# HGRN scores on TensorE: decay levels that share one loaded weight in pairs

## The reference, cut to what matters

```python
b = jnp.cumsum(lf_i, axis=1)
diff = b[:, :, None] - b[:, None, :]                 # decay from frame s to frame t
diff = jnp.where(tri[None, :, :, None, None], diff, -jnp.inf)
att = jnp.einsum('bthd,btshd->bhts', q_i, jnp.exp(diff) * k_i[:, None])
intra = jnp.einsum('bhts,bshe->bthe', att, v_i)
```

## Time and profile before

| | |
|---|---|
| Median of 3 runs | 2650.66 us (2640.95 to 2654.57) |
| Span of the profiled execution | 2647.1 us |
| PE busy | 2570.6 us (97%) |
| DVE / ACT / POOL busy | 1246.3 / 673.9 / 458.7 us |
| Mean granted TensorE clock | 0.988 |
| Idle time of PE before line 738 with DVE's ATT as releaser | 22.4 us in 11 places |

### The profile page before, as it was taken

How to read it: one execution, slowest core, us unless ns; L and a number is a source line. 1 busy time by engine, 2 the same in 40 slices (tenths; PEclk the granted TensorE clock), 3 DMA queues, 4 the chain that set the end, 5 groups by cost and what they waited for, 6 DMA issues and landing times.

```text
span 2647.1 us, 38662 instructions
## 1 busy us (share of the span) xinstructions
PE 2570.6 (97%) x14936; PEld 2453.3 (93%) x14936; DVE 1246.3 (47%) x2290; ACT 673.9 (25%) x1257; POOL 458.7 (17%) x680
## 2 busy tenths in 40 slices
PE   7999999999999999999999999999999999999998
PEld 6999999999999989999999999987998998998997
DVE  4043424325366566666576534455433333333335
ACT  5123222322212212222222233233221221221221
POOL 1011102002153353363364300001100000000000
PEclk9999999999999999999999999999999999999999
DMA  4251615234243223223133353322210110110114
GB/s 152 92 178 60 221 60 188 96 116 158 68 141 121 85 89 108 95 92 118 65 112 122 108 197 118 125 88 80 64 48 24 55 48 24 55 48 24 55 40 151
DMA packets 219034, 257.27 MB, mean 97 GB/s; under 512 B 8208, under 2 KB 186640, under 8 KB 218768
## 3 DMA queue, kind: packets, MB, share of 16 engines
q1 hardware_dynamic: 218896, 255.31, 28.9%
HBM read 175.06 MB, written 80.22 MB: 96 GB/s over the span
## 4 chain that ended last, share of the span: by engine, by line
PE 80%; DVE 11%; issue 6%; ACT 1%; DMA 1%; POOL 1%; SPq 0%; DVEq 0%; POOLq 0%; ACTq 0%
PE bank L585 11%; PE bank L587 11%; PE bank L586 11%; PE bank L832 5%; PE bank L833 5%; PE bank L834 5%; PE bank L903 5%; PE bank L901 5%; PE bank L902 5%; DVE QE L1375 3%; DVE PP L1376 3%; PE bank L746 3%; PE bank L862 1%; PE bank L861 1%; PE bank L860 1%
## 5 line engine op out<-in xcount | busy, mean ns | idle before, releaser
L585 PE MATMUL bank<-XH,WHI 128*128 128x384 f32 x2304 | 797.3, 346 | 22.3 <-issue 13.3
L587 PE MATMUL bank<-XH,WLO 128*128 128x384 f32 x2304 | 778.6, 338 | 0.0
L586 PE MATMUL bank<-XL,WHI 128*128 128x384 f32 x2304 | 778.1, 338 | 0.0
L585 PEld LDWEIGHTS bank<-XH,WHI 128*128 128x128 f32 x2304 | 439.7, 191 | 29.0 <-issue 14.0
L586 PEld LDWEIGHTS bank<-XL,WHI 128*128 128x128 f32 x2304 | 439.9, 191 | 1.1
L587 PEld LDWEIGHTS bank<-XH,WLO 128*128 128x128 f32 x2304 | 438.2, 190 | 0.0
L917 ACT ACTIVATE ZST<-bank 128x384 f32<-128x384 f32 x240 | 117.9, 492 | 843.3 <-PE bank L587 842.6
L1211 DVE TENSOR_TENSOR WLO<-WRAW,WHI 128x1024 fp32r<-128x1024 f32 x128 | 170.3, 1331 | 223.6 <-ACT WHI L917 218.4
L832 PE MATMUL bank<-XH,WHI 128*128 128x384 f32 x768 | 257.5, 335 | 3.6 <-ACT XH L917 3.6
L834 PE MATMUL bank<-XH,WLO 128*128 128x384 f32 x768 | 257.3, 335 | 0.0
L833 PE MATMUL bank<-XL,WHI 128*128 128x384 f32 x768 | 257.3, 335 | 0.0
(11 more groups left out here) (180 smaller groups left out, 3421.6 us busy)
## 6 DMA issues: line engine op xcount, KB each, us to landing
scratch_z<-ZST SPq DMA_DIRECT2D x80, 576.0 KB, 2.8
WRAW<-in_w_in SPq DMA_DIRECT2D x80, 512.0 KB, 4.2
HZ<-scratch_z SPq DMA_DIRECT2D x32, 576.0 KB, 4.9
WRAW<-in_w_up SPq DMA_DIRECT2D x32, 512.0 KB, 4.0
WRAW<-in_w_down SPq DMA_DIRECT2D x32, 512.0 KB, 3.2
MG<-scratch_z SPq DMA_DIRECT2D x16, 576.0 KB, 5.7
ZQ<-scratch_z SPq DMA_DIRECT2D x4, 1152.0 KB, 6.7
ZK<-scratch_z SPq DMA_DIRECT2D x4, 1152.0 KB, 8.6
```

Source lines behind the costliest of these rows:

```text
L585: pe.matmul(psum[c][:, 0:CH], WHI[p][:, k, :], XH[:, k, s], start=(k == 0), stop=False)
L586: pe.matmul(psum[c][:, 0:CH], WHI[p][:, k, :], XL[:, k, s], start=False, stop=False)
L587: last = pe.matmul(psum[c][:, 0:CH], WLO[p][:, k, :], XH[:, k, s], start=False, stop=(k == KT - 1))
```

## The change

PE: `KE` keeps four weights instead of seven: for levels 0 and 1 together, 2 and 3 together, 4 and 5 together, and 6. The lower level of a pair uses the weight as it is. At the upper level the sources in the first quarter of the block miss the decay over the second quarter; so Q has two versions there, one for each half of the sources, and the second is the first times that decay (kept in `FS`). The diagonal's matmul takes only the even frames (64 columns with step 2), since the weight of levels 0 and 1 at an odd frame is K itself. Moving widths in a tile are 64, 128, 192, 192 and 64 columns (in the last tile 64, 128 and 192). The pair of levels 4 and 5 goes to bank PT right behind the transposes, and `H.t_full` is raised after it, before the other score matmuls.

DVE: `prep_q` copies Q for level 0 instead of multiplying it, adds a small copy to FS at levels 2 and 4 (24 and up to 6 elements), makes it wait for the product before PP is updated, and adds a product `qa` at levels 3 and 5. `weights` takes nine sources of scores instead of eight (eight COPY_PREDICATED after the base instead of seven; in the last tile still four), with a new table MB in place of the identity, and doesn't wait for `H.kv` in the last tile.

POOL: `prep_k` makes the weights of levels 1, 2 and 4 over all 384 (or 256) columns and waits for each, that of level 6 over half as before, and none at levels 0, 3 and 5. SP loads one more table at the start, and the first group's inputs of the next stage in two DMAs more.

```diff
@@ constants @@
+KES = 4
+QES = 9
@@ tiles @@
-        KE = [sb(f"KE{i}", [P, LEV, CH], F32, ph) for i in range(2)]
+        KE = [sb(f"KE{i}", [P, KES, CH], F32, ph) for i in range(2)]
+        UAX = [sb(f"UAX{i}", [P, 3, CH], F32, ph) for i in range(2)]
-        QE = [sb(f"QE{i}", [P, LEV, CH // 2], F32, ph) for i in range(2)]
+        QE = [sb(f"QE{i}", [P, QES, CH // 2], F32, ph) for i in range(2)]
+        FS = sb("FS", [P, 32], F32, ph)
@@ hg_a @@
-                tr = pe.transpose(PT[:, P:2 * P], KRH[:, s], ident[:, :])
-                if t == NT - 1:
-                    tr.then_inc(H.t_full, 1)
-                last = pe.matmul(PSC[:, 0:P], KK[:, s], HZ[0][:, s], start=True, stop=True, skip_group_check=True)
                 kt = slice(r * P, (r + 1) * P)
                 qt = slice(r * 64, (r + 1) * 64)
-                for l in range(min(6, LEV if t < NT - 1 else LEVS)):
-                    last = pe.matmul(PSC[:, P + 64 * l:P + 64 * (l + 1)], KE[c % 2][:, l, kt], QE[c % 2][:, l, qt],
-                                     start=True, stop=True, skip_group_check=True)
+                last = pe.transpose(PT[:, P:2 * P], KRH[:, s], ident[:, :])
+                if t < NT - 1:
+                    last = pe.matmul(PT[:, 2 * P:2 * P + 192].rearrange("p (l n) -> p l n", l=3), KE[c % 2][:, 2, kt],
+                                     QE[c % 2][:, 5:8, qt], start=True, stop=True, skip_group_check=True)
+                last.then_inc(H.t_full, 1)
+                pe.matmul(PSC[:, 0:64], KK[:, s], HZ[0][:, t * P:(t + 1) * P:2], start=True, stop=True,
+                          skip_group_check=True)
+                last = pe.matmul(PSC[:, 64:192].rearrange("p (l n) -> p l n", l=2), KE[c % 2][:, 0, kt],
+                                 QE[c % 2][:, 0:2, qt], start=True, stop=True, skip_group_check=True)
+                last = pe.matmul(PSC[:, 192:384].rearrange("p (l n) -> p l n", l=3), KE[c % 2][:, 1, kt],
+                                 QE[c % 2][:, 2:5, qt], start=True, stop=True, skip_group_check=True)
+                if t < NT - 1:
+                    last = pe.matmul(PSC[:, 384:448], KE[c % 2][:, 3, kt], QE[c % 2][:, 8, qt], start=True, stop=True,
+                                     skip_group_check=True)
                 last.then_inc(H.sc, 1)
-                if t < NT - 1:
-                    last = pe.matmul(PT[:, 2 * P:2 * P + 64], KE[c % 2][:, 6, kt], QE[c % 2][:, 6, qt], start=True, stop=True)
-                    last.then_inc(H.t_full, 1)
@@ prep_q @@
-                    q = QE[c % 2][:, l, 0:n // 2].rearrange("p (g w) -> p g w", w=w)
+                    j = (0, 1, 2, 3, 5, 6, 8)[l]
+                    qa = QE[c % 2][:, j + 1, 0:n // 2].rearrange("p (g w) -> p g w", w=w) if l in (3, 5) else None
+                    q = QE[c % 2][:, j, 0:n // 2].rearrange("p (g w) -> p g w", w=w)
                     pp = v(PP)
-                    dve.tensor_tensor(q, v(HZ[0])[:, :, 1, :], pp[:, :, 1, :], ALU.mult)
+                    if l in (2, 4):
+                        dve.tensor_copy(FS[:, 12 * l - 24:12 * l - 24 + n // (4 * w)], PP[:, c * CH + 2 * w - 1:c * CH + n:4 * w])
+                    if l in (2, 4):
+                        ch(dve.tensor_tensor(q, v(HZ[0])[:, :, 1, :], pp[:, :, 1, :], ALU.mult))
+                    elif l:
+                        dve.tensor_tensor(q, v(HZ[0])[:, :, 1, :], pp[:, :, 1, :], ALU.mult)
+                    else:
+                        dve.tensor_copy(q, v(HZ[0])[:, :, 1, :])
                     ch(dve.tensor_tensor(pp[:, :, 1, :], pp[:, :, 1, :],
                                          pp[:, :, 0, w - 1:w].to_broadcast([P, n // (2 * w), w]), ALU.mult))
+                    if l in (3, 5):
+                        fs = FS[:, 12 * l - 36:12 * l - 36 + n // (2 * w)]
+                        dve.tensor_tensor(qa, q, fs.unsqueeze(2).to_broadcast([P, n // (2 * w), w]), ALU.mult)
@@ weights @@
-                dve.wait_ge(H.kv, 9 * h + t + 2)
+                if t < NT - 1:
+                    dve.wait_ge(H.kv, 9 * h + t + 2)
-                ch(dve.tensor_tensor(at[:, :], PSC[:, 0:P], ident[:, :], ALU.mult))
-                for l in range(LEV if t < NT - 1 else LEVS):
-                    w = 1 << l
-                    src = PSC[:, P + 64 * l:P + 64 * (l + 1)] if l < 6 else PT[:, 2 * P:2 * P + 64]
+                ch(dve.tensor_tensor(at[:, :].rearrange("p (g a) -> p a g", a=2),
+                                     PSC[:, 0:P].rearrange("p (a g) -> p a g", a=2), MB[:, :, :], ALU.mult))
+                for j in (1, 2, 3, 4, 8, 5, 6, 7) if t < NT - 1 else (1, 2, 3, 4):
+                    w = 1 << (0, 1, 2, 3, 3, 4, 5, 5, 6)[j]
+                    x = 64 + 64 * j
+                    src = PSC[:, x:x + 64] if j < 5 else PSC[:, 384:448] if j == 8 else PT[:, x - 128:x - 64]
...
@@ prep_k @@
-                    pool.tensor_tensor(v(KE[c % 2][:, l, :])[:, :, 0, :], v(KK[:, s])[:, :, 0, :], rr[:, :, 0, :], ALU.mult)
+                    if l in (1, 2, 4):
+                        ch(pool.tensor_tensor(KE[c % 2][:, l // 2, 0:n], KK[:, c * CH:c * CH + n], RR[:, c * CH:c * CH + n],
+                                              ALU.mult))
+                    elif l == 6:
+                        pool.tensor_tensor(v(KE[c % 2][:, 3, :])[:, :, 0, :], v(KK[:, s])[:, :, 0, :], rr[:, :, 0, :],
+                                           ALU.mult)
```

More of the change, by code:

```diff
@@ L119, in program @@
         ones = sb("ones", [P, P], F32, pa)
-        MK = sb("MK", [P, LEV, 64], U32, pa)
+        MK = sb("MK", [P, QES - 1, 64], U32, pa)
+        MB = sb("MB", [P, 2, 64], F32, pa)
         RM = sb("RM", [P, NS], F32, pa)
@@ L162, in program @@
         UA = [[HZ[k // NC][:, k % NC * CH:(k % NC + 1) * CH] for k in range(KT - 1)] + [URAW[:, :]]] + \
-            [[KE[i][:, k, :] for k in range(LEV)] + [HZ[2][:, (i + 1) * CH:(i + 2) * CH]] for i in range(2)]
+            [[KE[i][:, k, :] for k in range(KES)] + [UAX[i][:, k, :] for k in range(3)] +
+             [HZ[2][:, (i + 1) * CH:(i + 2) * CH]] for i in range(2)]
         ph.close()
@@ L384, in _ @@
             sp.dma_start(MK[:, :, :], a["c_mask"]).then_inc(c_in2, 16)
+            sp.dma_start(MB[:, :, :], a["c_base"]).then_inc(c_in2, 16)
             sp.dma_start(RM[:, :], a["c_rows"]).then_inc(c_in2, 16)
@@ L456, in load_ua @@
                     cs = slice(c * CH, (c + 1) * CH)
-                    sp.dma_start(KE[c - 1][:, :, :], us[0:LEV, :, cs].rearrange("k p t -> p k t")).then_inc(ua_in[c], 16)
-                    sp.dma_start(UA[c][LEV], us[LEV, :, cs]).then_inc(ua_in[c], 16)
+                    sp.dma_start(KE[c - 1][:, :, :], us[0:KES, :, cs].rearrange("k p t -> p k t")).then_inc(ua_in[c], 16)
+                    sp.dma_start(UAX[c - 1][:, :, :], us[KES:KT - 1, :, cs].rearrange("k p t -> p k t")).then_inc(ua_in[c], 16)
+                    sp.dma_start(UA[c][KT - 1], us[KT - 1, :, cs]).then_inc(ua_in[c], 16)
             ret_mixed(sp)
@@ L1053, in kz_hg @@
                     act.activation(KM8[b], PT[:, P:2 * P], ACT.Copy, scale=RM[:, b:b + 1]).then_inc(H.kz8, 1)
-            act.wait_ge(c_in2, 48)
+            act.wait_ge(c_in2, 64)
             def forget(h):
@@ L1065, in piece @@
                 if i < 3 * KT:
-                    act.wait_ge(ua_in[c], 32 if c else 64)
+                    act.wait_ge(ua_in[c], 48 if c else 64)
                     copy(XH[:, k, cs], UA[c][k]).then_inc(sp_hi, 1)
@@ L1315, in rotate_k0 @@
                 ch(dve.tensor_tensor(KR[:, 0, s], RTMP[:, 0, :], RTMP[:, 1, :], ALU.subtract))
-            dve.wait_ge(c_in2, 48)
+            dve.wait_ge(c_in2, 64)
             with dve.Fori(0, RH) as h:
@@ L1385, in weights @@
                 dve.wait_ge(H.st_full, 10 * h + (t if t >= 2 else 1))
-                dve.wait_ge(H.kv, 9 * h + t + 2)
+                if t < NT - 1:
+                    dve.wait_ge(H.kv, 9 * h + t + 2)
                 at = ATT[t % 2]
-                ch(dve.tensor_tensor(at[:, :], PSC[:, 0:P], ident[:, :], ALU.mult))
-                for l in range(LEV if t < NT - 1 else LEVS):
-                    w = 1 << l
-                    src = PSC[:, P + 64 * l:P + 64 * (l + 1)] if l < 6 else PT[:, 2 * P:2 * P + 64]
+                ch(dve.tensor_tensor(at[:, :].rearrange("p (g a) -> p a g", a=2),
[4 more added lines that the diff above has]
+                    src = PSC[:, x:x + 64] if j < 5 else PSC[:, 384:448] if j == 8 else PT[:, x - 128:x - 64]
                     g = lambda x: x.rearrange("p (g w) -> p g w", w=w)
                     last = dve.copy_predicated(at[:, :].rearrange("p (g a w) -> p g a w", a=2, w=w)[:, :, 1, :],
-                                               g(MK[:, l, :]), g(src))
-                    if l < (LEV if t < NT - 1 else LEVS) - 1:
+                                               g(MK[:, j - 1, :]), g(src))
+                    if j != (7 if t < NT - 1 else 4):
                         ch(last)
@@ L1615, in gate @@
```

(16 more changed lines are left out.)

## The result

The changed kernel takes 2673.65 us (median of 4 runs, 2673.16 to 2675.95), the kernel before 2649.06 us (median of 4 runs, 2640.95 to 2654.57): ratio 1.0098, 95% interval 1.0077 to 1.0118. The profiled execution has a span of 2671.4 us, 24.3 us longer. PE is busy for less (2548.1 us against 2570.6), as it was meant to be, and waits for more.

A forecast was written before the change was run, and what follows sets the result against it. PE was taken to bound most of a head, DVE slot 13 to tile 1. +26 us over eight heads and +10 for the clock made +36, so 2686 us; own range 2664 to 2710, overall 2638 to 2714.

The forecast's parts named there:

- What bounds the kernel: HGRN stage: PE bounds most of a head, but from slot 13 to tile 1 DVE sets the pace.
- PE's part: Score matmuls on PE: 0.43 us saved a tile, 0.32 in a head's last, 30 us in all.
- Rival 4: Score matmuls on PE: the wide ones gain nothing, +17 us, 2703 us; chance 0.05.
- DVE's part, c = 0 and 1: prep_q on DVE, first two groups: added products, tiny copies and waits cost 1.8 us a call.
- I count that as even: prep_k on POOL: 1.0 us less a call, but each of three wider products holds DVE longer; no net effect.
- Slot 13 to tile 1: DVE's stretch of a head: two prep_q calls 3.6 us plus one predicated copy 0.28, +3.9 us.
- Tile 4 to 5: Stretch of a head where DVE's longer prep_q part and merge decide: 8.9 us against 7.46, +1.45 us.
- sum by head: Changes of a head's five stretches added: +3.2 us a head, times 8 heads +26 us.
- The clock: Half clock behind PE's longer waits before tile 1 and at the stage's start: +10 us, bounds +2 and +25.
- The sum: Whole kernel: +26 us from the heads and +10 from the clock, +36 us on the span.
- the forecast's own range: Whole kernel: 2664 to 2710 us, from 1.0 to 2.6 us a prep_q call and clock +5 to +18.
- Rival 1: Prep stretches: DVE and POOL act as one queue, a call grows 0.3 us instead of 1.8; 2643 us, chance 0.17.

The follow-up runs named there:

- experiment 1: Changed kernel without the copies to FS, the products qa and the two waits that it adds to prep_q on DVE: 2636.0 us, ratio 0.9952.
- experiment 3: Changed kernel with POOL's prep_k(h, 1) held back until DVE has finished prep_q(h, 1): 2619.04 us, ratio 0.9890.
- 5: Kernel before, with the second part of prep_q(h, 1) moved from slot 1 to slot 4, behind the merge of tile 1: 2612.52 us, ratio 0.9862.
- experiment 2: Kernel before with only the DVE instructions added to prep_q, products into a scratch tile: 2688.93 us, ratio 1.0151.
- experiment 6: Changed kernel with the second part of prep_q(h, 1) moved from slot 1 to slot 4, behind the merge of tile 1: 2613.44 us, ratio 0.9863.
- (8): Changed kernel with POOL's prep_k(h, 1) held back and prep_q(h, 2) and slot 6's weight split rearranged behind merges in slots 5 to 7: 2595.81 us, ratio 0.9797.
- (9): Kernel before with POOL's prep_k(h, 1) held back and prep_q(h, 2) and slot 6's weight split rearranged behind merges in slots 5 to 7: 2612.38 us, ratio 0.9873.

## Why the prediction was right, point by point

- **What bounds the kernel.** Right. DVE's chain from slot 13 to tile 1 sets the head. This stretch makes 2.6 of the 4.5 us a head that experiment 1 takes off, 5.1 of 6.9 in experiment 3, 3.0 of 4.8 in 5, and 2.4 of the 5.4 that experiment 2 adds; most of the rest is the half clock behind it and tiles 4 and 5.
- **PE's part.** Predicted 0.43 us a tile and 0.32 in the last, measured 0.44 (tile 2 to 3 was 880.16 - 873.32 = 6.84 us, and is 6.40) and 0.34: 31 us for 30. Rival 4 (wide matmuls gain nothing) is out.
- **DVE's part, c = 0 and 1.** Predicted 3.6 us in both calls, measured in head 1 1.2 (12.3 to 13.5) and 2.6 (9.6 to 12.2), 3.8, and 3.5 in the mean of heads 1 to 7. The sum was right, its parts less so, and that they cancel is in part luck. The products `qa` took what was put on them (L1401, 0.607 us). The tiny copies took 0.56 us in the mean of these calls instead of 0.25, since a copy also stands behind POOL. The copy in place of level 0's product, put at -0.1, took 0.73 us where the product had 0.65. Against that, some old products got shorter (L1392, which now stands behind a copy, 0.355 us in the mean where L1375 had 0.610). I read this as DVE's sequence meeting POOL's in another order, so that only the sum of a call can be carried over; no run varies the order alone.

```profile
L1390 DVE COPY FS<-PP 128x24 f32<-128x24 f32 x24 | 16.6, 693 | 0.8
L1401 DVE TENSOR_TENSOR QE<-QE,FS 128x192 f32<-128x192 f32 x40 | 24.3, 607 | 1.4
L1392 DVE TENSOR_TENSOR QE<-HZ,PP 128x192 f32<-128x192 f32 x40 | 14.2, 355 | 0.0
```

- **"I count that as even"** (POOL's fewer but wider products). Nearly right: by experiment 1 the calls are as long with wide products as with narrow ones (21.5 and 21.6 us); by experiment 2 the wide ones cost at most 0.8 us a head more.
- **Slot 13 to tile 1**, +3.9 predicted, +3.4 measured. The two calls grew by 3.5 of the 3.6 us, and the merge by 0.2 and not 0.28 us: eight COPY_PREDICATED take 2.15 us where seven took 1.95. What the rest went to isn't shown; the kernel before has heads of 29.6 to 34.0 us here, and the changed one 34.1 to 35.4. This is the smaller of two mis-sized terms.
- **Tile 4 to 5**, +1.45 predicted, +0.8 measured. The mis-sized step is part 1 of c = 2: it grew from 4.5 to 5.4 us (894.37 to 899.81), by 1.0 and not 1.25 us. The merge grew less, as above, and two of the seven heads had a wait of 0.4 us here already, which the sum by head 1 didn't count.
- **The clock**, +10 predicted. What half clock cost can be read against the same stretches without it (tile 1 to 2: 6.65 us before, and 6.18 in experiment 6, since the changed kernel has none without it; tile 5 to 8: 20.44 after). Over heads 0 to 7 it cost 12.2 us before, all of it behind tile 1, and 16.6 behind tile 1 and 6.4 behind tile 5 after: +10.8. So the size was right, but not the place: the prediction put all of it behind tile 1 and at the stage's start. The rise came less behind tile 1 (+4.4), where in the longer waits part of the half clock falls on a PE that stands, than behind the new waits before tile 5 in four heads (+6.4). A reading was wrong too: four of the eight waits before tile 1 had no half clock behind them (1.65, 2.64, 0.61 and 2.09 us), not three, since one of the five stretches stands at the stage's start (757.6 to 764.4 us).
- **The sum.** +36 predicted, +24.6 measured (2673.65 - 2649.06), inside the forecast's own range; PE's wait for the merged scores came to 64 us, not to about 75. Since the clock's term came out, nearly all that is missing stands in the sum by head: 3.2 us predicted, 2.9 measured with the clock in it, and 1.7 without (8.6 of the clock's 10.8 us fall on heads 1 to 7). Rival 1, even or slightly faster by the shared access, had the access right but not its effect: DVE's two calls grew by 3.5 us, although POOL had less to do: POOL ended its `prep_k` for c = 1 0.9 to 6.1 us behind DVE's call before the change, and ends it 0.4 to 2.0 us ahead of it now. The rival's working was also off: 4 x 0.2 less 1.0 is -0.2, not the 0.3 us a call that it went on with.

## What to carry to other kernels

Before a change that trades matmuls for vector instructions, look for the place at which PE waits with the same releaser in every head. What the other engine gets in addition there is paid at once (here 3.4 us a head for 3.7 us of added work), whatever the busy shares (PE 97%, DVE 47%) say. Then look at whether two engines prepare for the same deadline at the same time: here POOL's work for the second group was done 11 to 21 us before PE needed it at tile 3, and still 4 to 7 us before with the hold; holding it back was worth 37 us without the change and 55 us with it. A change that loses by its side effects can be worth keeping once these are scheduled away (-16.6 us here, (8) against (9)).

## What the runs showed of the hardware

- A DVE copy of 6 elements a partition took 0.17 us with POOL idle and 0.98 us with POOL working (head 1); `prep_q`'s 20 instructions took 6.4 and 12.2 us. POOL lost less by the overlap: its whole `prep_k` for that group took 13.1 us beside `prep_q` and 11.8 with the hold, and its 384-column product 1.00 to 1.18 us in either case.
- A float32 matmul of 192 moving columns over a 128 x 128 weight took 0.32 us, of 64 columns 0.17 us between wide ones, against 0.215 us in a row of 64-column ones. The trace gives a hint why: the weight load of a matmul behind a 192-column one starts 0.15 us before it (881.75 and 881.90), behind a 64-column one 0.05 us before it (874.99 and 875.04). So it may pay to put narrow matmuls between wide ones; no run here tests the order by itself.
- A moving operand with a step of 2 elements cost nothing at 64 columns: 0.17 us, as the 64-column matmul without a step in the same tile.
